# Hybrid decoder step: the fourth prompt tile's final addition on ScalarE and GpSimd, and the decode tokens first in four partition groups

## The reference

```python
def rms_norm(x, g):
    xf = x.astype(jnp.float32)
    xf = xf * lax.rsqrt(jnp.mean(jnp.square(xf), axis=-1, keepdims=True) + RMS_EPS)
    return (xf * g.astype(jnp.float32)).astype(x.dtype)

def swiglu(hn, w_gate, w_up, w_down):
    return (jax.nn.silu(hn @ w_gate) * (hn @ w_up)) @ w_down

y_p = y_p + rms_norm(swiglu(hp, w_gate[l], w_up[l], w_down[l]), g_ffn_post[l])
y_s = y_s + rms_norm(swiglu(hs, w_gate[l], w_up[l], w_down[l]), g_ffn_post[l])
```

## Time and profile before

| what | value |
| --- | --- |
| time, median of 3 runs | 987.44 us (986.85 to 987.71) |
| the profiled execution | 986.85 us |
| its span, first to last instruction | 984.7 us |
| TensorE busy | 939.9 us, 95% of the span |
| VectorE, ScalarE, GpSimd busy | 443.1, 356.2, 171.0 us |
| chain that ended last | TensorE 84%, VectorE 8%, ScalarE 3% |

### The profile page before, as it was taken

The page is one execution under the profiler, slowest core; times in us unless marked ns, Lnnn a source line. Parts: engine busy times, 40 slices in busy tenths (PEclk is TensorE's granted clock), DMA queues, the critical chain, the costliest instruction groups (busy, mean ns, idle before and its releaser), DMA issues.

```text
span 984.7 us, 18139 instructions
## 1 busy us (share of the span) xinstructions
PE 939.9 (95%) x7738; PEld 874.4 (89%) x7738; DVE 443.1 (45%) x900; ACT 356.2 (36%) x565; POOL 171.0 (17%) x46
## 2 busy tenths in 40 slices
PE   3999999899899999999989999999999999999997
PEld 2999997676699999976569999999999999999996
DVE  5899975765354687121553572222222222001103
ACT  5443124564453464225424543222222222222111
POOL 3000000000000001300030003333333333353330
PEclk9999999989999999999999999999999999999999
DMA  7304205332152357449051111222223322222202
GB/s 214 114 29 130 87 2 200 127 125 87 50 176 81 109 177 270 173 178 377 2 171 44 43 39 49 85 85 87 89 95 94 95 94 75 86 76 75 87 33 91
DMA packets 85344, 105.85 MB, mean 108 GB/s; under 512 B 9474, under 2 KB 72835, under 8 KB 85155
## 3 DMA queue, kind: packets, MB, share of 16 engines
q1 hardware_dynamic: 85056, 104.92, 32.1%
q10 hardware_dynamic: 226, 0.05, 0.0%
HBM read 98.26 MB, written 6.70 MB: 107 GB/s over the span
## 4 chain that ended last, share of the span: by engine, by line
PE 84%; DVE 8%; ACT 3%; issue 2%; DMA 1%; ACTq 0%; DVEq 0%
PE pall L1795 56%; PE pall L1807 6%; PE pall L2129 5%; PE pall L1832 3%; PE pall L2180 2%; PE pall L1819 1%; PE pall L2199 1%; DVE a_s L1433 1%; PE pall L1868 1%; PE pall L2235 1%; PE pall L1994 1%; PE pall L1985 1%; PE pall L1885 1%; DMA out_new_k_prompt<-k_tok 1%; PE pall L1851 1%
## 5 line engine op out<-in xcount | busy, mean ns | idle before, releaser
L626 POOL TENSOR_TENSOR w_lo<-w_raw,w_hi 128x2048 fp32r<-128x2048 f32 (+1 forms) x36 | 161.2, 4477 | 621.2 <-ACT w_hi L669 331.5
L1795 PE MATMUL pall<-x_hi,w_hi 128*128 128x272 f32 x1024 | 213.1, 289 | 0.0
L1795 PE MATMUL pall<-x_lo,w_hi 128*128 128x272 f32 x1024 | 211.5, 288 | 0.0
L1795 PE MATMUL pall<-x_hi,w_lo 128*128 128x272 f32 x1024 | 210.4, 287 | 0.0
L1795 PEld LDWEIGHTS pall<-x_lo,w_hi 128*128 128x128 f32 x1024 | 161.1, 189 | 0.0
L1795 PEld LDWEIGHTS pall<-x_hi,w_hi 128*128 128x128 f32 x1024 | 159.9, 188 | 0.7
L1795 PEld LDWEIGHTS pall<-x_hi,w_lo 128*128 128x128 f32 x1024 | 160.4, 188 | 0.0
L669 ACT ACTIVATE w_hi<-w_raw 128x2048 fp32r<-128x2048 f32 (+1 forms) x61 | 114.6, 1879 | 91.7 <-PE pall L1795 91.2
L1795 PE MATMUL pall<-g_hi,w_hi 128*128 128x272 f32 x352 | 73.1, 289 | 0.0
L1795 PE MATMUL pall<-g_lo,w_hi 128*128 128x272 f32 x352 | 72.7, 288 | 0.0
L1795 PE MATMUL pall<-g_hi,w_lo 128*128 128x272 f32 x352 | 72.6, 287 | 0.0
(11 more groups left out here) (387 smaller groups left out, 1636.7 us busy)
## 6 DMA issues: line engine op xcount, KB each, us to landing
w_raw<-in_w_gate SPq DMA_DIRECT2D x10, 1024.0 KB, 5.4
w_raw<-in_w_up SPq DMA_DIRECT2D x10, 1024.0 KB, 5.3
w_raw<-in_w_in SPq DMA_DIRECT2D x8, 1024.0 KB, 7.0
w_raw<-in_w_down SPq DMA_DIRECT2D x8, 1024.0 KB, 5.0
dm_kv<-in_cache_mem_v SPq DMA_DIRECT2D x5, 1024.0 KB, 13.5
w_raw<-in_w_out SPq DMA_DIRECT2D x4, 1024.0 KB, 6.1
d_k<-in_cache_k SPq DMA_DIRECT2D x16, 256.0 KB, 2.9
d_v<-in_cache_v SPq DMA_DIRECT2D x16, 256.0 KB, 3.9
```

Of the source, the lines that this page charges most:

```text
L626: e.tensor_tensor(w_lo[:, n % 2, 0:w], w_raw[:, n % 2, 0:w], w_hi[:, n % 2, 0:w].bitcast(F32), ALU.subtract)\
L1795: ins = mm(acc(j)[:, a, :], w, x[:, k_x + k, a * HALF:(a + 1) * HALF], start=first and k == 0 and s_, stop=last and k == kts - 1 and t_)
```

## The change

It does four things, and renames some semaphores to make room.

- **Tile 3.** Its residual is transposed after the first unit of the down projection, into banks 6 and 7, and ScalarE copies it from there to a new tile `y_res`. At the end ScalarE multiplies tile 3 by the reciprocal root, and GpSimd adds `y_res`; SP stores tile 3 between tiles 1 and 2.
- **Tile 0.** Its residual is transposed between the two last groups of `zg` transposes instead of behind them.
- **Decode tokens.** Their part of `zg` is turned by an ordinary matmul with `zg` as the weights, and lands on partitions 32 (k % 4) and up, so that the 1024 columns become 256 on all 128 partitions. The residual and the sums of squares are laid out alike. The decode addition is the first of VectorE's four, over 256 columns; the decode result leaves in four stores of 32 partitions, ahead of the prompt tiles.
- **Roots.** One root and one reciprocal over five columns in the place of two each.
- **Semaphores.** `eps_ready` and `x_ms` become one, `subln_sq` joins `att_oT`; so in the mixer part the sums of the last head (`head_sums`) wait for the square of the decode part too.

```diff
@@ y_banks
-        b = (0, 2, 6, 0, 2)[t]
+        b = (0, 2, 6, 6)[t]
@@ sync (SP)
-        for t in range(5):
-            e.wait_ge(S("y_ready"), t + 1)
-            if t < 4:
-                store(out_y[t], y_tok[:, t, :])
-            else:
-                store(O["y_sample"].rearrange("b t d -> (b t) d"), y_tok[0:NS_TOK, t, :])
+        e.wait_ge(S("y_ready"), 1)
+        for q in range(4):
+            store(O["y_sample"].rearrange("b t (j q c) -> q (b t) j c", j=2, q=4)[q],
+                  y_tok[32 * q:32 * q + 32, 4, 0:256].rearrange("p (j c) -> p j c", j=2))
+        for t in (0, 1, 3, 2):
+            e.wait_ge(*((S("y3_ready"), 1) if t == 3 else (S("y_ready"), t + 2)))
+            store(out_y[t], y_tok[:, t, :])
@@ gpsimd, behind the last split_lo
+        e.wait_ge(S("y3_res"), 2)
+        e.tensor_tensor(y_tok[:, 3, :], y_tok[:, 3, :], y_res[:], ALU.add).then_inc(S("y3_ready"), 1)
@@ scalar, in the down projection
+            if n == U_DOWN + 1:
+                e.wait_ge(S("yT_full"), 1)
+                e.activation(y_res[:], y_banks(3), ACT.Copy).then_inc(S("y3_res"), 1)
@@ scalar, end
-        e.activation(small[:, Y_RSTD:Y_RSTD + 4], bank(4)[:, 0:4], ACT.Sqrt, ...)
-        e.activation(small[0:NS_TOK, Y_RSTD + 4:Y_RSTD + 5], bank(4)[0:NS_TOK, 4:5], ACT.Sqrt, ...)
+        e.activation(small[:, Y_RSTD:Y_RSTD + 5], bank(4)[:, 0:5], ACT.Sqrt, ...)
+        e.wait_ge(S("zgT_out"), 2 * KT)
+        e.wait_ge(S("norm_recip"), 6)
+        e.activation(y_tok[:, 3, :], y_tok[:, 3, :], ACT.Copy, scale=small[:, Y_RSTD + 3:Y_RSTD + 4]).then_inc(S("y3_res"), 1)
@@ vector
-                e.tensor_copy(y_tok[0:NS_TOK, 4, k * P:(k + 1) * P], bank(b + 1)[0:NS_TOK, 0:P]).then_inc(S("zgT_out"), 1)
+                rows = slice(32 * (k % 4), 32 * (k % 4) + 32)
+                e.tensor_copy(y_tok[rows, 4, k // 4 * P:(k // 4 + 1) * P], bank(b + 1)[rows, 0:P]).then_inc(S("zgT_out"), 1)
@@
-        for t in range(5):
-            rows = P if t < 4 else NS_TOK
-            e.wait_ge(S("yT_full"), t + 1)
+        for i, t in enumerate((4, 0, 1, 2)):
+            cols, res = (D, y_banks(t)) if t < 4 else (256, bank(5)[:, 0:256])
+            e.wait_ge(S("yT_full"), (3, 2, 4, 5)[i])
@@ tensor, zg_transposes
+                elif k == 1:
+                    e.wait_ge(S("y3_res"), 1)
...
-                e.transpose(bank(b + 1)[0:NS_TOK, 0:P], zg[:, k % 2, NP_TOK:TOK], ident[:]).then_inc(S("zgT_full"), 1)
+                mm(bank(b + 1)[32 * (k % 4):32 * (k % 4) + 32, 0:P], zg[:, k % 2, NP_TOK:TOK], ident[:], start=True, stop=True).then_inc(S("zgT_full"), 1)
+                if k == KT - 2:
+                    y_transposes(0)
@@ tensor, loop over the units
+            if n == U_DOWN:
+                y_transposes(3)
@@ tensor, end
-        for t in range(5):
-            w = P if t < 4 else NS_TOK
-            ins = mm(bank(4)[0:w, t:t + 1], sqacc[:, t * P:t * P + w], ones[:, 0:1], start=True, stop=True)
+        for t in range(4):
+            mm(bank(4)[:, t:t + 1], sqacc[:, t * P:(t + 1) * P], ones[:, 0:1], start=True, stop=True)
+        for q in range(4):
+            ins = mm(bank(4)[32 * q:32 * q + 32, 4:5], sqacc[:, NP_TOK:TOK], ones[:, 0:1], start=True, stop=True)
         ins.then_inc(S("norm_sum"), 1)
-        e.wait_ge(acc_out, J_DOWN + KT)
+        for k in range(KT):
+            rows = slice(32 * (k % 4), 32 * (k % 4) + 32)
+            ins = mm(bank(5)[rows, k // 4 * P:(k // 4 + 1) * P], yT[:, k, NP_TOK:TOK], ident[:], start=True, stop=True)
+        ins.then_inc(S("yT_full"), 1)
         y_transposes(1)
         e.wait_ge(S("zgT_out"), 2 * KT)
         y_transposes(2)
-        for t in (3, 4):
-            e.wait_ge(S("y_ready"), t - 2)
-            y_transposes(t)
```

More of the change, by code:

```diff
@@ L1086, in _ @@
         e.wait_ge(*counted("n5", "sum", 1))
[L1087 to L1089 removed]
+        e.activation(small[:, Y_RSTD:Y_RSTD + 5], bank(4)[:, 0:5], ACT.Sqrt, bias=small[:, EPS_COL:EPS_COL + 1]).then_inc(S("norm_root"), 1)
+        e.wait_ge(S("zgT_out"), 2 * KT)
+        e.wait_ge(S("norm_recip"), 6)
+        e.activation(y_tok[:, 3, :], y_tok[:, 3, :], ACT.Copy, scale=small[:, Y_RSTD + 3:Y_RSTD + 4]).then_inc(S("y3_res"), 1)
     @block.vector
@@ L1146, in split_lo @@
             lo_done[0] += 1
-        e.memset(small[:, EPS_COL:EPS_COL + 1], EPS).then_inc(S("eps_ready"), 1)
+        e.memset(small[:, EPS_COL:EPS_COL + 1], EPS).then_inc(S("x_eps_ms"), 1)
         for t in SQ_DVE:
@@ L1155, in _ @@
         e.wait_ge(S("x_ss"), 5)
-        e.tensor_scalar(small[:, 8:12], small[:, 0:4], 1.0 / D, EPS, ALU.mult, ALU.add).then_inc(S("x_ms"), 1)
-        e.tensor_scalar(small[0:NS_TOK, 12:13], small[0:NS_TOK, 4:5], 1.0 / D, EPS, ALU.mult, ALU.add).then_inc(S("x_ms"), 1)
+        e.tensor_scalar(small[:, 8:12], small[:, 0:4], 1.0 / D, EPS, ALU.mult, ALU.add).then_inc(S("x_eps_ms"), 1)
+        e.tensor_scalar(small[0:NS_TOK, 12:13], small[0:NS_TOK, 4:5], 1.0 / D, EPS, ALU.mult, ALU.add).then_inc(S("x_eps_ms"), 1)
         e.wait_ge(S("x_root"), 1)
@@ L1529, in _ @@
                 e.wait_ge(S("x_ss"), 5 + 2)
-                e.tensor_scalar(small[:, 8:10], small[:, 0:2], 1.0 / D, EPS, ALU.mult, ALU.add).then_inc(S("x_ms"), 1)
+                e.tensor_scalar(small[:, 8:10], small[:, 0:2], 1.0 / D, EPS, ALU.mult, ALU.add).then_inc(S("x_eps_ms"), 1)
                 e.wait_ge(S("x_root"), 1 + 1)
@@ L1759, in _ @@
                 e.tensor_copy(y_tok[:, 0:4, k * P:(k + 1) * P], bank(b).rearrange("p (t c) -> p t c", t=4)).then_inc(S("zgT_out"), 1)
-                e.tensor_copy(y_tok[0:NS_TOK, 4, k * P:(k + 1) * P], bank(b + 1)[0:NS_TOK, 0:P]).then_inc(S("zgT_out"), 1)
-        e.wait_ge(*counted("n5", "root", 2))
-        e.reciprocal(small[:, Y_RSTD:Y_RSTD + 4], small[:, Y_RSTD:Y_RSTD + 4])
-        done(e.reciprocal(small[0:NS_TOK, Y_RSTD + 4:Y_RSTD + 5], small[0:NS_TOK, Y_RSTD + 4:Y_RSTD + 5]))
-        e.wait_ge(S("zgT_out"), 2 * KT)
-        for t in range(5):
-            rows = P if t < 4 else NS_TOK
-            e.wait_ge(S("yT_full"), t + 1)
-            e.scalar_tensor_tensor(out=y_tok[0:rows, t, :], in0=y_tok[0:rows, t, :], scalar=small[0:rows, Y_RSTD + t:Y_RSTD + t + 1],
-                                   in1=y_banks(t)[0:rows, :], op0=ALU.mult, op1=ALU.add).then_inc(S("y_ready"), 1)
+                rows = slice(32 * (k % 4), 32 * (k % 4) + 32)
+                e.tensor_copy(y_tok[rows, 4, k // 4 * P:(k // 4 + 1) * P], bank(b + 1)[rows, 0:P]).then_inc(S("zgT_out"), 1)
+        e.wait_ge(*counted("n5", "root", 1))
+        e.reciprocal(small[:, Y_RSTD:Y_RSTD + 5], small[:, Y_RSTD:Y_RSTD + 5]).then_inc(S("norm_recip"), 1)
+        e.wait_ge(S("norm_recip"), 6)
+        e.wait_ge(S("zgT_out"), 2 * KT)
+        for i, t in enumerate((4, 0, 1, 2)):
+            cols, res = (D, y_banks(t)) if t < 4 else (256, bank(5)[:, 0:256])
+            e.wait_ge(S("yT_full"), (3, 2, 4, 5)[i])
+            e.scalar_tensor_tensor(out=y_tok[:, t, 0:cols], in0=y_tok[:, t, 0:cols], scalar=small[:, Y_RSTD + t:Y_RSTD + t + 1],
+                                   in1=res, op0=ALU.mult, op1=ALU.add).then_inc(S("y_ready"), 1)
     @block.tensor
@@ L2056, in _ @@
                 head_sums(3)
-                e.wait_ge(S("subln_sq"), 1)
+                e.wait_ge(S("att_oT"), NH)
                 for h in range(NH):
@@ L2313, in _, with y_transposes @@
                     product(m, slot, 256, m * P, x_hi, x_lo, 0, KT).then_inc(acc_full, 1)
+        def y_transposes(t):
+            for k in range(KT):
+                ins = e.transpose(y_banks(t)[:, k * P:(k + 1) * P], yT[:, k, t * P:(t + 1) * P], ident[:])
+            ins.then_inc(S("yT_full"), 1)
         def zg_transposes(c):
```

19 lines of the change are left out of this document (8 added, 11 removed).

## The result

The changed kernel takes 991.70 us, median of 7 runs (989.67 to 994.67), against 987.44 before (7 runs, 983.68 to 988.13). The ratio is 1.0046, with a 95% interval of 1.0032 to 1.0060: slower by 3.2 to 5.9 us. The forecast was 989.4, in a range from 988.0 to 991.0. The sign of the sum was right and its size was not.

A forecast was written before the change was run, and what follows sets the result against it. It took full TensorE in the down projection, then the first large store's start plus saturated transfers, as the bounds. +0.87 + 0.65 - 0.24 + 0.67 = +1.95 us gave 988.8 profiled, 989.4 with 0.6 for the median; range 988.0 to 991.0.

The forecast's parts named there:

- Part 1: Down projection: tile 3's eight transposes, without a TensorE gap to hide in, add 0.87 us; ScalarE's copy is free.
- Part 2: Zg blocks in the down projection: each decode matmul adds a second record of 0.109 us; six make +0.65 us.
- The bounds: Zg decode matmuls in the projection: between 0, if second records overlap their neighbours, and 0.65 us, the value taken.
- Part 3: Last product to first final addition: earlier sums, one root and reciprocal, but a wait for the decode residual; -0.24 us.
- Part 4: Final stores: four decode stores at SP's 1.81 us delay the first prompt store; end +0.67 us after first addition starts.
- collision: Final additions: VectorE contends with GpSimd's tile 3 addition, tile 1 waits, the queue starves some 1.7 us; 991.1, chance 0.07.
- slow start: First prompt tile's store: data start late behind four small stores, price 0.4 to 0.8 us; about 990.0, chance 0.20.
- Cheap issues: Decode stores: SP issues each in 0.34 us without gaps, for a sum of +1.5 us; 988.9, chance 0.14.
- stores that don't bind: Kernel's end: it follows the last addition instead of the transfers, net -0.7 us; 986.8, chance 0.08.
- merged semaphores: Near the start: no cost, since the narrow square the head sums also await ends before the last wide one starts.

The follow-up runs named there:

- b_zg_wide: Kernel before, decode part of zg turned by matmuls with 128-column weights, decode output wrong; weight split after first down unit's seam to last squaring 112.14 us, 0.66 more.
- a_groups_contiguous: Changed kernel with decode columns laid out so each of the four decode stores is a plain 32 x 256; 990.56 us, ratio 1.0042 to the kernel before.
- a_decode_plain: Changed kernel without its decode part: decode on 32 partitions, turned by transposes, added and stored last in one store; 986.84 us, ratio 0.9994 to the kernel before.
- a_stores_last: Changed kernel with the four decode stores issued behind the prompt stores on SP; 992.07 us, ratio 1.0059 to the kernel before.
- b_zg_matmul: Kernel before with one edit: decode part of zg turned by an ordinary matmul on the same partitions 0 to 31; 989.59 us, ratio 1.0016.

## Why the prediction was right or wrong

**Part 1, tile 3 in the projection: right.** +0.91 against +0.87, from the seam; ScalarE's copy was hidden as said.

**Part 2, decode part of zg by matmul: wrong, and the largest miss.** +2.40 against +0.65. The step that failed is the price of the decode matmul, a second record of 0.109 us, taken from a row of full-width transposes. It holds for a wide matmul (b_zg_wide, +0.66). For the narrow one it was 0.40 us, 2.40 for six: TensorE's weight loads pause ahead of it and behind it, 0.37 us together, and the second record itself adds only some 0.03. The bounds failed with it: they reached below the value taken and not above, since nothing there allowed for a cost per change.

**Part 3, the way to the first addition: right in sum by luck, wrong in its steps.** -0.18 against -0.24 (its terms, 974.81 + 0.52 + 0.27 + 0.05, add up to 975.65 and so to -0.19). The forecast took the decode residual as the last to arrive; by the chain of sums, root and reciprocal alone it had -0.43. Measured, the residual's 16 records lasted 0.62, where 0.52 + 0.27 was worked out, and ended at 978.22, before the reciprocal's end at 978.31: they did not bound T, the chain did, and it was 0.25 us longer than forecast. The sums started 976.53 - 973.99 = 2.54 us behind S2, where 973.48 - 971.26 = 2.22 was said. VectorE's copy of k = 6, for which they wait, ended 976.13 + 0.29 - 973.99 = 2.43 behind S2 instead of 2.17 (why, see below), and TensorE would hardly have been free sooner: its narrow matmul of k = 7 started at 976.07, and such a one kept full-width work away for 0.34. The single reciprocal saved nothing: from its start to T are 0.27 us, before 0.25 for two, where 0.10 less was said. What made most of it good again is the eight narrow sums: they lie in four groups, and the next matmuls, narrow too, follow them after 977.60 - 977.51 = 0.09 us, not 0.34. The pause of 0.20 comes only behind the residual, where T doesn't wait for it.

**Part 4, decode first in four stores: right mechanism, mis-sized.** +1.55 against +0.67. Of the difference of 0.88, 0.87 are SP's four issues, 2.68 us instead of 1.81. The step that failed is the price of SP's issue, 0.45 us each, read from two-dimensional transfers; for these stores it was 0.67. a_groups_contiguous shows 0.45 right for plain ones. Behind the first large store the forecast held: 10.41 - 3.19 = 7.22 us to the end, as worked out. That VectorE's shorter queue brings nothing against saturated transfers is what a_decode_plain shows.

**The rivals.** No collision: the four additions took 4.06 us, 0.4 and three times 1.2, beside GpSimd's 2.35 from 979.64 (2.4 was worked out); the two that started in that time, at 979.98 and 981.17, lasted 1.27 each, as in the kernel before. The trace agrees with the Trainium skill's rule on the port (SBUF — State Buffer, "Who interferes with whom") for the form with a scalar column too. No slow start either: with the first large store issued at 981.58, the transfers are at 410 GB/s in the slice from 982.75. The Trainium skill's rule on transfers under 64 KB (DMA: Bandwidth & Descriptors, "Measured (HBM→SBUF, 128 partitions, SWDGE, issued from GpSimd)") had made the slow start likelier; the trace doesn't show one, and the time was lost at the issue. Cheap issues are refuted by SP's row, and stores that don't bind by a_decode_plain.

**Noise.** The forecast lay 0.6 us above the profiled sum, for the median of the runs; the size of what runs differ by ahead of S0, several us, was not in the range. That the merged semaphores cost nothing was not tried by itself: a_decode_plain has them too, and its whole shows no loss, within 0.3%.

## What to carry to other kernels

Price an instruction that is added to a full TensorE stream by its form and its neighbours, not by its record count: a narrow matmul between full-width transposes cost 0.40 us more than the narrow transpose in its place, a wide one 0.11 more. Keep tiny stores plain in shape and out of the way of the first large one, since a queue that is saturated afterwards never gives the delay back. And where one engine's work and the transfers behind it run at nearly the same rate, shortening one alone buys nothing; look first which of them has reserve.

## What the runs showed of the hardware

- Around a matmul with weights of 32 columns and 128 moving columns, TensorE's weight loads paused for 0.17 us ahead, where full-width transposes stood in front of it, and for 0.20 us behind, before full-width work. Transposes of the same shape, matmuls with weights of 128 columns, and narrow matmuls with one moving column (full-width work behind them) did not.
- Eight narrow sums in four partition groups took 0.09 us until the next, also narrow, matmul started, while eight in one group took 0.34 until a full-width one did; their weight loads took 0.16 and 0.33.
- SP needed 0.67 us for a store of 32 x 2 x 128 and 0.45 for one of 32 x 256 with nothing large in flight, and 0.95 for one of 32 x 2 x 128 behind four large stores (a_stores_last).
- VectorE's copies start later where their first partition changes. A wide copy and the narrow one behind it were 0.60 us apart with both at partition 0, and 0.73 with the narrow one at partition 64 or 96:

```profile
975.10 0.68 DVE L1759 COPY y_tok<-pall 128x512 f32<-128x512 f32 x1
975.70 0.27 DVE L1760 COPY y_tok<-pall 32x128 f32<-32x128 f32 x1
```

  in b_zg_matmul, and in the changed kernel

```profile
975.40 0.69 DVE L1768 COPY y_tok<-pall 128x512 f32<-128x512 f32 x1
...
976.13 0.29 DVE L1771 COPY y_tok<-pall 32x128 f32<-32x128 f32 x1
976.51 0.69 DVE L1768 COPY y_tok<-pall 128x512 f32<-128x512 f32 x1
...
977.24 0.30 DVE L1771 COPY y_tok<-pall 32x128 f32<-32x128 f32 x1
```

The Trainium skill (VectorE: DVE Perf Modes, "Two Vector instructions with no wait between them") has a model for this: an instruction whose inputs or output start in another group of 32 partitions than the last ones did is held until all earlier ones have finished. The trace agrees: 975.40 + 0.69 = 976.09, and the narrow copy starts at 976.13, where the one at partition 0 started 0.08 us before its forerunner's end.
